# Two transformer blocks on one core: norms over seven summed chunks with earlier signals, and another order at the mixers' ends

## The reference

```python
def layer_norm(x, g, b):                       # first block
    mu = jnp.mean(xf, axis=-1, keepdims=True)
    var = jnp.mean(jnp.square(xf - mu), axis=-1, keepdims=True)
    return ((xf - mu) * lax.rsqrt(var + LN_EPS)) * g + b
# first block, each layer: FFN + norm, attention + norm, FFN + norm
def _rms_norm(x, gain):                        # second block
    return xf * lax.rsqrt(jnp.mean(xf * xf, axis=-1, keepdims=True) + EPS) * gain
# second block, each layer
x = x + 0.5 * _swiglu(_rms_norm(x, ffn1_norm[l]), ffn1_wi[l], ffn1_wo[l])
u = _rms_norm(x, mix_norm[l]);  c = _split_cols(u @ w_in[l] + b_in[l])
y_sb  = stick-breaking attention of c           # 4 heads of 64
y_ml  = _mlstm(...)                             # matrix memory in 2 chunks of 128, 4 heads of 128
y_mla = _mla(...)                               # latent attention, 4 heads
x = x + (gates * (y_sb @ w_up_sb, y_ml @ w_up_ml, y_mla @ w_up_mla)).sum() @ w_out[l]
x = x + 0.5 * _swiglu(_rms_norm(x, ffn2_norm[l]), ffn2_wi[l], ffn2_wo[l])
```

## Time and profile before

| | us |
|---|---|
| time before, median of 3 runs | 2771.67 (2766.2 to 2775.52) |
| the profiled execution's own time | 2773.23 |
| its span in the profile | 2771.5 |
| PE busy, share of the span | 2634.9 (95%) |
| DVE busy | 1632.2 (59%) |
| ACT busy | 1100.8 (40%) |
| POOL busy | 343.2 (12%) |
| granted TensorE clock, mean | 0.975 of full speed |

### The profile page before, as it was taken

The page is one execution under the profiler, slowest core; times in us unless marked ns, Lnnn a source line. Parts: engine busy times, 40 slices in busy tenths (PEclk is TensorE's granted clock), DMA queues, the critical chain, the costliest instruction groups (busy, mean ns, idle before and its releaser), DMA issues.

```text
span 2771.5 us, 41112 instructions
## 1 busy us (share of the span) xinstructions
PE 2634.9 (95%) x16160; PEld 2269.8 (82%) x16160; DVE 1632.2 (59%) x2365; ACT 1100.8 (40%) x1545; POOL 343.2 (12%) x408
## 2 busy tenths in 40 slices
PE   6999998999899998999998999989899999998999
PEld 3888886867688886888887689979889999997989
DVE  4665746566574574575655755565565566575555
ACT  3221224265421223321224753444555444455443
POOL 3000022122300003200012020010001100000210
PEclk8999999999999999999999999999899999998999
DMA  6553533421253351354442035535324454431544
GB/s 244 170 177 130 195 108 129 160 68 47 90 192 129 114 191 67 137 189 137 166 141 91 30 137 177 202 136 194 111 92 147 162 200 160 166 139 71 183 164 148
DMA packets 64252, 394.24 MB, mean 142 GB/s; under 512 B 7440, under 2 KB 8944, under 8 KB 29040
## 3 DMA queue, kind: packets, MB, share of 16 engines
q1 hardware_dynamic: 41072, 308.78, 31.8%
q0 software_dynamic: 21344, 77.41, 8.4%
q10 hardware_dynamic: 1696, 6.08, 0.6%
HBM read 391.19 MB, written 1.05 MB: 142 GB/s over the span
## 4 chain that ended last, share of the span: by engine, by line
PE 84%; DVE 8%; ACT 4%; issue 2%; DMA 1%; POOL 1%; ACTq 0%; POOLq 0%; DVEq 0%
PE banks L412 24%; PE banks L414 24%; PE banks L413 24%; DVE wlo L377 3%; ACT whi L369 2%; PE banks L437 1%; PE banks L1043 1%; PE banks L439 1%; PE banks L438 1%; PE banks L1067 1%; PE banks L1054 1%; DMA shift_start<-in_w_mod 1%; PE banks L427 1%; PE banks L428 1%; PE banks L429 1%
## 5 line engine op out<-in xcount | busy, mean ns | idle before, releaser
L377 DVE TENSOR_TENSOR wlo<-raw,whi 128x2048 fp32r<-128x2048 f32 (+1 forms) x272 | 668.3, 2457 | 463.5 <-ACT whi L369 463.5
L369 ACT CAST whi<-raw 128x2048 fp32r<-128x2048 f32 (+1 forms) x272 | 548.4, 2016 | 252.8 <-PE banks L414 212.2
L412 PE MATMUL banks<-uhi,whi 128*128 128x512 f32 (+1 forms) x1648 | 602.5, 366 | 3.5 <-DVE wlo L377 3.5
L414 PE MATMUL banks<-uhi,wlo 128*128 128x512 f32 (+1 forms) x1648 | 600.3, 364 | 0.0
L413 PE MATMUL banks<-ulo,whi 128*128 128x512 f32 (+1 forms) x1648 | 600.1, 364 | 0.0
L412 PE MATMUL banks<-u2hi,whi 128*128 128x256 f32 x1312 | 374.8, 286 | 6.8 <-DVE wlo L377 4.3
L413 PE MATMUL banks<-u2lo,whi 128*128 128x256 f32 x1312 | 370.9, 283 | 0.0
L414 PE MATMUL banks<-u2hi,wlo 128*128 128x256 f32 x1312 | 370.7, 283 | 0.0
L412 PEld LDWEIGHTS banks<-uhi,whi 128*128 128x128 f32 x1648 | 309.8, 188 | 60.3 <-DVE wlo L377 4.1
L414 PEld LDWEIGHTS banks<-uhi,wlo 128*128 128x128 f32 x1648 | 309.9, 188 | 55.5
L413 PEld LDWEIGHTS banks<-ulo,whi 128*128 128x128 f32 x1648 | 310.0, 188 | 55.1
(11 more groups left out here) (382 smaller groups left out, 3904.0 us busy)
## 6 DMA issues: line engine op xcount, KB each, us to landing
raw<-in_ffn_in SPq DMA_DIRECT2D x132, 1024.0 KB, 4.8
raw<-in_ffn_out SPq DMA_DIRECT2D x48, 1408.0 KB, 6.2
mod_slot<-in_w_mod POOLq DMA_DIRECT2D x128, 512.0 KB, 3.6
raw<-in_w_merge SPq DMA_DIRECT2D x32, 1024.0 KB, 4.8
raw<-in_w_in SPq DMA_DIRECT2D x26, 1024.0 KB, 4.8
raw<-in_na_qkv SPq DMA_DIRECT2D x12, 1024.0 KB, 4.8
raw<-in_w_out SPq DMA_DIRECT2D x8, 1024.0 KB, 4.7
raw<-in_wa_qkv SPq DMA_DIRECT2D x6, 1024.0 KB, 4.7
```

The costliest lines, as they stand in the source:

```text
L369: act.copy(whi[u % 2][:, 0:unit_size[u]], raw[u % 2][:, 0:unit_size[u]]).then_inc(hi_done, 1)
L377: dve.tensor_tensor(wlo[u % 2][:, 0:n], raw[u % 2][:, 0:n], whi[u % 2][:, 0:n].bitcast(F32), ALU.subtract).then_inc(lo_done, 1)
L412: pe.matmul(out, w_hi, x_hi[:, k, 0:T], start=(n == 0), stop=False)
L414: mm = pe.matmul(out, w_lo, x_hi[:, k, 0:T], start=False, stop=(n == len(chunks) - 1))
```

## The change

1. **Sums.** GpSimd adds seven chunks, not six, to each running sum. TensorE's `means_pe` makes two products for each bank, not three, and signals the mean by itself before the mean square.
2. **Signals.** VectorE raises a signal after the first half of the last unit, and chunk 6 is ready by it. ScalarE waits for "mean" before it squares the mean; VectorE waits for "means" as well before the variance.
3. **ScalarE's order in the last unit of a projection ahead of a norm.** The table load stands ahead of the squares of chunk 6; outside the folded norms, the early `split_hi` stands between the squares of chunks 6 and 7, no longer behind both. In norms 9, 10 and 12 the table load stands behind the two high parts and ahead of the squares, and the early split stays behind them. Norm 7 has no table load of its own any more.
4. **Mixers' ends.** On all three engines the first latent steps move ahead of the matrix memory's carried part, and `ml_features` moves behind the last scores.

`CENTRED_EARLY = 4` is the old `KC // 2` under a name.

```diff
     def sums_pool(pool, s, T, source, mean):
-        for cc in range(KC - 2):
+        for cc in range(KC - 1):
...
     def means_pe(pe, s, T, source):
-        last = (KC - 2, KC - 1)
+        def mean_of(bank_, summed, x, ready):
+            pe.matmul(banks[:, bank_, 0:T], c("mean1024"), summed, start=True, stop=False)
+            pe.wait_ge(*ready)
+            return pe.matmul(banks[:, bank_, 0:T], c("mean1024"), x, start=False, stop=True)
         if source is not None:
-            means(4, [(POOL_.at("sum", s, KC - 3), sums[:, 0, 0:T])] + [(source(cc), h[:, cc, 0:T]) for cc in last])
-        means(5, [(POOL_.at("sq sum", s, KC - 3), sums[:, 1, 0:T])]
-              + [(ACT_.at("sq", s, cc), squares[:, cc % 2, 0:T]) for cc in last]).then_inc(*PE_.up(("means", s)))
+            pe.wait_ge(*POOL_.at("sum", s, KC - 2))
+            mean_of(4, sums[:, 0, 0:T], h[:, KC - 1, 0:T], source(KC - 1)).then_inc(*PE_.up(("mean", s)))
+        pe.wait_ge(*POOL_.at("sq sum", s, KC - 2))
+        mean_of(5, sums[:, 1, 0:T], squares[:, (KC - 1) % 2, 0:T], ACT_.at("sq", s, KC - 1))\
+            .then_inc(*PE_.up(("means", s)))
...
     def rstd_act(act, s, T, mean):
-        if s in TAKES and s != 7:
+        if s in FOLDED and s != 7:
             split_hi(act, TAKES[s].u0 + 1, early=True)
-        act.preload_act_table_set("natural_log_exp_and_others")
-        act.wait_ge(*PE_.at("means", s))
         if mean:
+            act.wait_ge(*PE_.at("mean", s))
...
     def centre_dve(dve, s, T):
         dve.wait_ge(*ACT_.at("mean2", s))
+        dve.wait_ge(*PE_.at("means", s))
...
     def last_evicted(ph):
-        return lambda cc: (evicted, ph.u0 + cc // 2 + 1)
+        return lambda cc: (DVE_.at("half of last unit", ph.u0) if cc == KC - 2 else (evicted, ph.u0 + cc // 2 + 1))
...
     def last_norm1_act(act, s):
-        split_hi(act, TAKES[s + 1].u0 + 1, early=True)
...
     def out_act(act, name, s=None, T=None):
-            if s is not None:
+            if s is None:
+                continue
+            if i < ph.n - 1:
                 squares_act(act, s, T, last_evicted(ph), (2 * i, 2 * i + 1))
+                continue
+            act.preload_act_table_set("natural_log_exp_and_others")
+            squares_act(act, s, T, last_evicted(ph), (KC - 2,))
+            if s not in FOLDED:
+                split_hi(act, (TAKES[s] if s in TAKES else TAKES[s + 1]).u0 + 1, early=True)
+            squares_act(act, s, T, last_evicted(ph), (KC - 1,))
...
     def out_dve(dve, name, T, gated_by, ready, s=None):
+                if half == 0 and i == ph.n - 1:
+                    ins.then_inc(*DVE_.up(("half of last unit", ph.u0)))
             ins.then_inc(evicted, 1)
```

More of the change, by code:

```diff
@@ L668, in rstd_act @@
         else:
+            act.wait_ge(*PE_.at("means", s))
             act.activation(var[:, 0:T], banks[:, 5, 0:T], ACT.Ln, bias=c("rms_eps")).then_inc(*ACT_.up())
@@ L671, in rstd_act @@
         act.activation(rstd[:, 0:T], var[:, 0:T], ACT.Exp, scale=-0.5).then_inc(*ACT_.up(("rstd", s)))
+    CENTRED_EARLY = 4
     def centre_dve(dve, s, T):
         dve.wait_ge(*ACT_.at("mean2", s))
+        dve.wait_ge(*PE_.at("means", s))
         dve.tensor_tensor(var[:, 0:T], banks[:, 5, 0:T], var[:, 0:T], ALU.subtract).then_inc(*DVE_.up())
@@ L677, in centre_dve @@
         dve.tensor_scalar(var[:, 0:T], var[:, 0:T], 0.0, None, ALU.max).then_inc(*DVE_.up(("var", s)))
-        for cc in range(KC // 2):
+        for cc in range(CENTRED_EARLY):
             centre_chunk(dve, s, T, cc)
@@ L761, in norm1_dve @@
                     .then_inc(*DVE_.up(("n", s, cc)))
-            if cc < KC // 2:
-                centre_chunk(dve, s, T, cc + KC // 2)
+            if cc < KC - CENTRED_EARLY:
+                centre_chunk(dve, s, T, cc + CENTRED_EARLY)
             if cc and s < 6:
@@ L806, in last_norm1_dve @@
                     .then_inc(*DVE_.up(("n", s, cc)))
-            if cc < KC // 2:
-                centre_chunk(dve, s, S, cc + KC // 2)
+            if cc < KC - CENTRED_EARLY:
+                centre_chunk(dve, s, S, cc + CENTRED_EARLY)
             if cc:
@@ L2026, in mix_pe @@
         ml_num_pe(pe, l)
-        ml_inter_pe(pe, l)
         mla_scores_pe(pe, l, 0)
         mla_scores_pe(pe, l, 1)
-        ml_features_pe(pe, l)
+        ml_inter_pe(pe, l)
+        mla_transposes_pe(pe, l, 0)
         mla_scores_pe(pe, l, 2)
-        mla_transposes_pe(pe, l, 0)
-        mla_scores_pe(pe, l, 3)
         mla_transposes_pe(pe, l, 1)
         mla_values_pe(pe, l, 0)
+        mla_scores_pe(pe, l, 3)
+        ml_features_pe(pe, l)
         mla_transposes_pe(pe, l, 2)
@@ L2107, in mix_act @@
         ml_state_act(act, l)
+        mla_exp_act(act, l, 0)
+        mla_exp_act(act, l, 1)
         ml_inter_act(act, l)
         ml_squares_act(act, l)
+        mla_probs_t_act(act, l, 0)
         ml_rms_act(act, l)
-        mla_exp_act(act, l, 0)
-        mla_exp_act(act, l, 1)
-        mla_probs_t_act(act, l, 0)
+        mla_probs_t_act(act, l, 1)
         mla_exp_act(act, l, 2)
-        mla_probs_t_act(act, l, 1)
+        mla_exp_act(act, l, 3)
+        mla_probs_t_act(act, l, 2)
         ml_y_act(act, l, 0)
-        mla_exp_act(act, l, 3)
         ml_y_act(act, l, 1)
-        mla_probs_t_act(act, l, 2)
         mla_y_act(act, l, 0)
@@ L2174, in mix_dve @@
         mla_k_dve(dve, l)
+        mla_max_dve(dve, l, 0)
+        mla_max_dve(dve, l, 1)
+        mla_probs_dve(dve, l, 0)
         ml_sum_dve(dve, l)
         ml_den_dve(dve, l)
-        mla_max_dve(dve, l, 0)
+        mla_probs_dve(dve, l, 1)
         ml_ss_dve(dve, l)
-        mla_max_dve(dve, l, 1)
+        mla_max_dve(dve, l, 2)
         ml_h_dve(dve, l)
-        mla_probs_dve(dve, l, 0)
-        mla_max_dve(dve, l, 2)
-        mla_probs_dve(dve, l, 1)
+        mla_max_dve(dve, l, 3)
+        mla_probs_dve(dve, l, 2)
         ml_y_dve(dve, l, 0)
-        mla_max_dve(dve, l, 3)
+        mla_probs_dve(dve, l, 3)
         ml_y_dve(dve, l, 1)
-        mla_probs_dve(dve, l, 2)
         ml_y_lo_dve(dve, l, 0)
-        mla_probs_dve(dve, l, 3)
         ml_y_lo_dve(dve, l, 1)
```

5 lines of the change are left out of this document (removed).

## The result

| | before | after |
|---|---|---|
| median of the runs, us | 2775.79 (18 runs, 2766.2 to 2788.5) | 2764.45 (18 runs, 2755.45 to 2768.25) |
| the profiled execution's own time | 2773.23 | 2767.41 |
| its span | 2771.5 | 2765.7 |
| granted TensorE clock, mean | 0.975 | 0.974 |

The ratio is 0.9949, with a 95% interval from 0.9936 to 0.9961. On the 2771.67 of the prediction's three runs that is 2757.5, 14.1 us less, where 2757.3 and 14.4 were forecast. But the two profiled executions are only 5.8 us apart. Much of what follows is about that gap.

The account below looks back on a forecast made before the run. It took TensorE's waits as the only time to win, with norms 1 to 4 bound by ScalarE's and VectorE's splits in series. 7.8 + 0.6 + 1.1 + 2.1 + 1.6 + 1.2 = 14.4 us: 2771.67 to 2757.3, range 2750 to 2766.

Parts of the forecast that it names:

- Norms 1 to 4: Early split starts with the last product's end, so TensorE starts 1.95 us earlier at each norm: 7.8 us.
- win nothing by themselves: Norms 1 to 4: two products less, about 1.7 us of TensorE, only make room for the later square.
- Norms 5 and 6: The 256-wide norms: split freed from the square ahead of it, 0.6 us in norm 5, 1.1 in norm 6.
- Norms 8 and 11: Split starts earlier and the table load leaves the path; the splits set the end: 1.05 us each, 2.1 together.
- Folded norms: Norms 7, 9, 10 and 12, table load moved or dropped: 1.6 us won together, bounds -1.5 (a loss) and 3.
- Mixers' ends: Latent steps ahead of the carried part: 0.6 us for each of two mixers, 1.2 together.
- The play of the queues: Mixers' ends: three engine queues played forward in both orders; new order 0.7 us earlier, good to about 1.5 each.
- The squares: Rival: chunk 7's square and adds end after VectorE's split, norms 1 to 4 win about 0.7 each: 2763.8 us, 7%.
- The table load: Rival: one more load before the logarithm; norms 8 and 11 win nothing, folded ones lose 0.8 each: 2762 us, 3%.
- The matrix memory: Rival at the mixers' ends: features come 4.6 us later, little hidden, 3 us lost per mixer: 2764.5 us, 8%.
- The mixers win more: Rival: 3 us won in each mixer because the latent chain is longer and starts 2 us earlier: 2752.5 us, 8%.
- The seventh adds: Rival: GpSimd's adds end late at every norm, 1.9 us lost at each of norms 1 to 4: 2782.9 us, 4%.

Follow-up runs that it names:

- e3: Kernel before plus ScalarE's new order alone (table load and early split moved), old sums, signal and mixers' ends: 2775.90 us, ratio 0.9986.
- e4: Kernel before plus seven-chunk sums and the two signals alone, ScalarE's order and mixers' ends as before: 2782.31 us, ratio 1.0010.
- e2: Kernel before plus the new order at the mixers' ends alone, norms as before: 2776.35 us, ratio 0.9995 to before.
- e1: Kernel before plus all edits except the new order at the mixers' ends: 2766.47 us against 2777.66, ratio 0.9957.
- e9: Changed kernel with one narrow product of the gates behind each wide one, not in a row: 2756.43 us, ratio 0.9925 to before.
- e10: Same as e9 but with the old order at the mixers' ends: 2762.50 us, ratio 0.9948 to before.
- e8: The changed kernel run again, nothing altered, to compare profile and runs: 2762.07 us.

## Why the prediction came out right, and where it did not

**Norms 1 to 4**, 7.8 forecast, 7.9 in the rows. The length is right, the reason given is incomplete. The prediction said that the norm "is bound by ScalarE's split and VectorE's split in series" and that the two products less "win nothing by themselves". The step that failed is the look at what else was late: it compared the last product's end, 424.48, with the variance, 425.15, and called the rest 0.67 of room. Between them stands ScalarE's square of the mean, which waited for the same signal. The timeline of before has it:
```profile
424.52 0.60 ACT L665 ACTIVATE sums<-banks 128x512 f32<-128x512 f32 x1 [0.38 <-PE banks L647]
```
It ends at 425.12, 0.03 ahead of the variance, so the two chains were tied. e3 and e4 show it: 0.37 and 0.58 each by itself, 1.97 together. Without the seventh chunk and the early signal of the mean only 0.37 of the 1.97 is won; the sum was right only because the change did both.

**Norms 5 and 6**, 0.6 and 1.1 forecast, 0.69 and 1.08 measured to the first product of `first_unit`. **Norms 8 and 11**, 1.05 each forecast, 1.05 measured.

**Folded norms**, 1.6 forecast, 1.2 measured to the start of the third unit: 0.53, 0.11, 0.44 and 0.12 in norms 7, 9, 10 and 12. (Norm 7 is counted from the first product behind norm 6.) In norm 7 the seventh adds do end last: TensorE waits 4.0 us for them (L644 behind L638), where it waited 3.1 in before for the sixth. The sign was right. Norm 7 lost one whole table load and won less than its 1.28, and in e3, which has lost the load too, nothing at all (22.5 us to the third unit, 22.2 to 22.5 in the three profiles of before); nothing here shows the drain that the Trainium skill ("ScalarE: Activation LUTs", What ACT_TABLE_LOAD costs) adds to each switch.

**Mixers' ends**, 1.2 forecast. This term was mis-sized. The play of the queues held for the case that the profile of before happened to show: there the new order wins 0.7 and 1.2, the scores start 1.5 behind the numerators, and the last low part is 0.7 earlier, all as forecast. It took for granted that TensorE's numerators are over ahead of VectorE's keys. In 20 of the 28 mixers they are not, and there the order wins about 3.2 a mixer. In the kernel before they are, in five of six; it is in the changed kernel, whose clock is lower ahead of them, that they come late. What that is worth in the runs is between: 1.3 us by e2 against before, 2.0 by after against e1, 6.1 by e9 against e10. That the first two are so much smaller than 6.4 is not settled; the stretches ahead of the numerators differ by up to 9 us between executions (113 to 122 us in the second mixer) and can bury it. In e2's second mixer that stretch took 121.3 us where before has 113.0.

**The sum.** By rows the norms give 13.0 and the mixers 1.9 to 6.4, so 15 to 19 us; the runs say 14.1, with an interval from 10.8 to 17.7. The two profiles say 5.8, because the profiled execution of before was a good one (2773.23, where 2778.1 is the median of its 56 runs beside the experiments) and after lost 5.7 us ahead of the first numerators and 8.8 ahead of the second to a lower clock. What is left, some 2 us, is spread over the rest and was not followed. The forecast matched the ratio closely, and some of that is luck: a tie that was not seen, a mixer term too small by 0.7 to 5.2, and a loss of 5 us and more by the clock ahead of most mixers' ends, which the sum does not have.

**The rivals.** The squares did not bind: the variance, at 421.86, follows VectorE's split. The table load stayed where it was put. The matrix memory did not bind: its features came 3.4 to 4.6 later and the merge earlier. "The mixers win more" is half true. The seventh adds bound at norm 7 alone.

## What to carry to other kernels

List every chain that feeds the step behind a stall, down to each small operation, and add them all up to the same point: two ends within 0.1 us are a tie, and half of a change wins little on it. A difference of two profiles is not a difference of two kernels; compare runs, and from the profiles take only stretches measured from an event that both share. Before moving work in a stretch of small products, look at the granted clock ahead of it, since how much an order wins can depend on which engine is late there. And look at the clock again behind the change: a stretch that starts earlier can go along with a loss in the next one.

## What was not expected of the hardware

In 56 runs of the kernel before the time goes with the mean granted clock of the run: 2785 to 2788 at 0.968, 2767 to 2768 at 0.978, by a straight line 2.0 us for each 0.001, and 2.1 us are left around it. TensorE's clock fell to 1.2 GHz not only behind idle time but in a full row of products of 8 columns, in 22 mixers of 22, and stayed there for 3 to 10 us, partly of wide ones; the same products, mixed one by one with those of 256 columns, left it at 2.4 GHz in 6 of 6 and made the kernel 7 us faster by the ratios (0.9949 to 0.9925), 8 by the medians. At norms 1 to 4 the low clock behind the idle time costs little. VectorE gives a chunk each 1.2 to 1.8 us and its products need 1.4 at 2.4 GHz, so TensorE catches up: in after the products of the last chunk start 0.05 to 0.25 us behind its low part. In e8, where the clock was low for 10 us at norm 2, they start 1.0 behind it.
